# Two moves in a two-block transformer kernel: one projection issued a stage earlier, and the order of the first loads

## The reference

```python
h = _rms(x, attn_norm_g[l])
...
fq = _rms(_heads(proj("fox_q"), FOX_HEADS), fox_q_norm_g[l])    # 16 heads of 64
fk = _rms(_heads(proj("fox_k"), FOX_HEADS), fox_k_norm_g[l])
fv = _heads(proj("fox_v"), FOX_HEADS)
y_fox = _merge_heads(_fox_attention(fq, fk, fv, log_f))         # softmax attention with decay

def _rg_lru_branch(x, gate, conv_w, conv_b, w_a, b_a, w_x, b_x, lam):
    xc = _causal_dwconv(x, conv_w, conv_b)                      # x = proj("lru_x"), 4 taps
    r = sigmoid(einsum('bsnd,nde->bsne', xg, w_a) + b_a)        # xg: xc in 16 blocks of 64
    i = sigmoid(einsum('bsnd,nde->bsne', xg, w_x) + b_x)
    log_a = -LRU_C * r * softplus(-lam)
    ...
    return hs * gelu(gate)                                      # gate = proj("lru_g")

mem_n = _rms(mem, mem_norm_g[l])                                # read by the memory branch
```

## Time and profile before

| | before |
|---|---|
| runs (us) | 3090.07, 3090.10, 3087.36; median 3090.07 |
| the profiled execution: its own time | 3087.68 |
| its span | 3085.9 |
| PE busy | 3031.9 us, 98% of the span |
| DVE busy | 1628.8 us, 53% |
| ACT busy | 671.7 us, 22% |
| granted TensorE clock, mean | 0.999 |

### The profile page before, as it was taken

The page is one execution under the profiler, slowest core; times in us unless marked ns, Lnnn a source line. Parts: engine busy times, 40 slices in busy tenths (PEclk is TensorE's granted clock), DMA queues, the critical chain, the costliest instruction groups (busy, mean ns, idle before and its releaser), DMA issues.

```text
span 3085.9 us, 41509 instructions
## 1 busy us (share of the span) xinstructions
PE 3031.9 (98%) x13922; PEld 2419.9 (78%) x13922; DVE 1628.8 (53%) x3317; ACT 671.7 (22%) x1609; POOL 66.7 (2%) x109
## 2 busy tenths in 40 slices
PE   9999999999999999999999999999999999999998
PEld 8888888888885566767775588888866778887887
DVE  4456236666763466768886264444343666653111
ACT  3334210010003333311113041110053431022001
POOL 0000001100110000000000000000000000000000
PEclk9999999999999999999999999999999999999999
DMA  5243457756761111112221212222211223433443
GB/s 190 97 149 109 144 203 266 265 195 225 259 232 55 43 43 55 53 66 82 82 82 61 95 36 94 88 82 89 88 55 43 79 70 124 155 116 120 152 159 107
DMA packets 105001, 363.26 MB, mean 118 GB/s; under 512 B 11488, under 2 KB 17632, under 8 KB 104800
## 3 DMA queue, kind: packets, MB, share of 16 engines
q1 hardware_dynamic: 90832, 310.92, 29.5%
q0 software_dynamic: 14096, 51.39, 4.7%
HBM read 361.21 MB, written 1.05 MB: 117 GB/s over the span
## 4 chain that ended last, share of the span: by engine, by line
PE 95%; DVE 2%; issue 1%; ACT 1%; DMA 0%; DVEq 0%; ACTq 0%; SPq 0%
PE bank L569 42%; PE bank L942 6%; PE bank L1350 5%; PE bank L1010 4%; PE bank L1234 4%; PE bank L1125 3%; PE bank L580 3%; PE bank L842 2%; PE bank L1248 2%; PE bank L954 2%; PE bank L1098 2%; PE bank L1293 1%; PE bank L859 1%; PE bank L805 1%; PE bank L597 1%
## 5 line engine op out<-in xcount | busy, mean ns | idle before, releaser
L569 PE MATMUL bank<-H,W 128*128 128x256 f32 (+1 forms) x3488 | 816.3, 392 | 2.9 <-issue 2.8
L569 PEld LDWEIGHTS bank<-H,W 128*128 128x128 f32 x3488 | 661.4, 190 | 136.1 <-issue 52.0
L569 PE MATMUL bank<-YG,W 128*128 128x256 f32 (+1 forms) x1856 | 481.4, 416 | 1.8 <-issue 1.5
L569 PEld LDWEIGHTS bank<-YG,W 128*128 128x128 f32 x1856 | 352.8, 190 | 112.2 <-issue 72.5
L1125 PE MATMUL bank<-H,W 128*128 128x512 f32 (+1 forms) x320 | 119.7, 510 | 2.5 <-ACT H L1746 2.5
L1234 PE MATMUL bank<-W,H 128*128 128x256 f32 x512 | 117.1, 379 | 0.0
L1234 PEld LDWEIGHTS bank<-W,H 128*128 128x128 f32 x512 | 95.0, 191 | 13.1 <-issue 1.9
L942 PE MATMUL bank<-MX,SQ 128*128 128x256 f32 x480 | 105.2, 379 | 0.0
L1453 ACT ACT_TABLE_LOAD x21 | 26.9, 1283 | 346.4 <-DVEq L305 338.4
L942 PEld LDWEIGHTS bank<-MX,SQ 128*128 128x128 f32 x480 | 91.4, 190 | 12.2
L1125 PEld LDWEIGHTS bank<-H,W 128*128 128x128 f32 x320 | 58.7, 190 | 45.5 <-issue 37.0
(11 more groups left out here) (453 smaller groups left out, 4431.1 us busy)
## 6 DMA issues: line engine op xcount, KB each, us to landing
W<-stream SPq DMA_DIRECT2D x556, 512.0 KB, 3.3
WORK<-ada POOLq DMA_DIRECT2D x59, 512.0 KB, 4.0
SQ<-ada POOLq DMA_DIRECT2D x28, 512.0 KB, 5.5
W<-stream SPq DMA_DIRECT2D x24, 384.0 KB, 3.5
YG<-ada POOLq DMA_DIRECT2D x9, 512.0 KB, 4.6
W<-stream SPq DMA_DIRECT2D x16, 128.0 KB, 2.5
CN<-consts SPq DMA_DIRECT2D x1, 1984.0 KB, 15.4
X<-x_in SPq DMA_DIRECT2D x2, 512.0 KB, 5.1
```

What stands on the lines that cost most here:

```text
L569: m = pe.matmul(out_ap, W[u][:, c, :], src[:, c, cols], start=first and c == 0, stop=last and c == k - 1)
```

## The change

Three things. On SP, the small load of lambda is issued after the two halves of `x` instead of before them. On PE, projection 0 of the first `lru_in` turn is issued in `fox_last`, behind the transposes and ahead of the value products. And the body of `lru_in` on PE is cut anew: a turn has projection 1 and the block matmuls, and at its end projection 0 of the turn that follows; the last turn stands behind the loop. Two waits are added (`q_taken`, `k_taken` of the phases before), which guard banks 0 and 1 across the phases. ACT's and DVE's programs are not touched.

```diff
@@ block.sync
             lam = slice(PCOL["lru_lam"], PCOL["lru_lam"] + KC)
-            sp.dma_start(PR[:, lam], params[:, lam]).then_inc(tally.sem("lam_loaded"), 16)
             for h in range(2):
                 sp.dma_start(X[:, 4 * h:4 * h + 4, XS], x_in[:, 4 * h:4 * h + 4, :]).then_inc(tally.sem(f"x_loaded{h}"), 16)
+            sp.dma_start(PR[:, lam], params[:, lam]).then_inc(tally.sem("lam_loaded"), 16)
             sp.dma_start(CN[:, 0:EARLY_CONSTS], consts[:, 0:EARLY_CONSTS]).then_inc(tally.sem("consts_loaded"), 16)
@@ fox(s), on PE
                 if s.attends:
                     soft_transpose(pe, s, 0, bank[6], FOX_MOVES, 0)
                     soft_transpose(pe, s, 1, bank[5], FOX_MOVES, 0)
+                if not s.projects:
+                    lru_first(Step(tally, plan, s.number + 1, 0, counting=False))
                 if s.projects:
                     pe.wait_ge(*s.before("rstd"))
...
-            def lru_in(s):
+            def lru_first(s):
+                pe.wait_ge(*s.earlier("q_taken", 0))
                 pe.wait_ge(*s.before("conv_done"))
                 project(s, 0, bank[0][:, 0:S], XS)
+
+            def lru_begin(s):
+                pass
+
+            def lru_middle(s, following):
+                lru_rest(s)
+                lru_first(following)
+
+            def lru_rest(s):
+                pe.wait_ge(*s.earlier("k_taken", 0))
                 pe.wait_ge(*s.before("gate_taken"))
                 project(s, 1, bank[1][:, 0:S], XS)
                 pe.wait_ge(*s.done("loaded2"))
...
-            run(pe, {"prepare": prepare, "fox": fox, "lru_in": lru_in,
+            run(pe, {"prepare": prepare, "fox": fox, "lru_in": (lru_begin, lru_middle, lru_rest),
```

## The result

The changed kernel takes 3093.99 us (median of 16 runs, 3092.17 to 3096.62); the kernel before, with more runs than were shown ahead, 3088.65 us (16 runs, 3087.18 to 3090.10). The ratio is 1.0018, 95% interval [1.0011, 1.0025]: 5.3 us between the medians, slower, and on the edge of the 0.2% that I took as the bound of what can be told. The profiled execution took 3093.96 us.

The account below looks back on a forecast made before the run. The prediction took PE as the bound, busy for 3031.9 of 3085.9 us. Its terms 1.7 + 2.4 + 0 made +4.1 us on a median of 3090.07, so 3094.1 us, with a range from 3088.8 to 3097.0.

Parts of the forecast that it names:

- Part 1: First loads: lambda lands behind x, holding up ACT's squares and DVE's casts, so the normalisation starts late; +1.7 us.
- DVE's chain: At the start: DVE's work from lambda's landing to the last cast, 5.84 us, now ending at 12.64, later than ACT's root.
- Rival A: First loads: lambda lands by itself within 1.8 us of issue, start wins 0.45, seam loses 2.4; +1.9 us, chance 0.10.
- Part 2: Seam of fox_last and lru_in: early projection 0 overfills the 1.07 us hole, delaying value products and block matmuls; +2.4 us.
- DVE's series: At the seam: DVE's output copies, memory normalisation, clearing and convolution, behind the value products, hold the block matmuls; moves by 2.38.
- Part 3: lru_in loop cut anew: same PE order, turns stay 7.77 us and the loop's edge costs nothing; 0 us.
- rival C: lru_in loop: seven edges and one exit each show a PE issue gap, 3.5 us; +7.6 us in all, chance 0.12.
- Rival B: Start and seam: x comes 0.45 us earlier, the moved projection holds nothing up, seam wins nothing; -0.45 us, chance 0.05.

Follow-up runs that it names:

- e7: Kernel before plus the change's PE part, loads as before, with DVE's memory normalisation ahead of the output copies of fox_last; 3086.96 us, ratio 0.9993.
- e4: Kernel before plus the change's PE part, loads as before, with 7 unused matmuls ahead of projection 1; 3090.45 us, ratio 1.0004.
- e12: As e4, with 3 unused matmuls instead of 7 ahead of projection 1; one run, 3092.65 us.
- e3: Kernel before with only the lru_in loop cut anew, projection 0 of turn 0 kept behind the value products; 3087.38 us, ratio 0.9996.
- e8: Kernel before with only DVE's memory normalisation moved ahead of its output copies in fox_last; 3088.11 us, ratio 0.9997.
- e6: Kernel before with lambda's load issued on ACT's own queue and x first on SP; 3088.68 us, ratio 0.9999.
- e1: Kernel before with only lambda's load moved behind both halves of x on SP; 3090.31 us, ratio 1.0004.
- e10: Changed kernel with DVE's memory normalisation moved ahead of its output copies in fox_last; 3088.86 us, ratio 1.0001.
- e11: Kernel before with lambda's load between the halves of x, second trial of that kernel; one run, 3090.26 us.
- e2: Kernel before plus the change's PE part (early projection 0 and loop cut anew), loads as before; 3092.52 us, ratio 1.0011.

## Why the prediction came out

**The time.** 3094.1 forecast, 3093.99 measured, within the range, and the class (within 0.2%) as forecast, if narrowly. But the agreement to 0.1 us is luck: the median of before that I started from lay 1.4 us above that of 16 runs, and the loss was 5.3 and not 4.1. The two differences cancel almost exactly.

**Part 1 was right in its mechanism.** Lambda landed at 1.81 + 4.83 = 6.64, forecast 6.8. DVE's chain needed its 5.84 us from there and set the normalisation, not the root. The term was forecast at +1.7 and measured at +1.38: 0.16 from the landing, and the rest from the gap that I left between the casts and the normalisation, where the trace has them overlap (12.40, ahead of the last cast's end at 12.48). Half 0 of `x` landed at 0.75 + 4.1 = 4.85 and not at 5.35; nothing hung on that, since ACT waited for lambda anyway. The Trainium skill ("DMA: Bandwidth & Descriptors", section "Queues, rings and completion order") states that each DMA engine takes the descriptors of a ring in order. The traces agree: on SP's queue lambda landed at 5.1 and 5.3 behind half a megabyte and at 6.6 to 6.7 behind a whole one, and at 3.3 and 4.1 on a queue of its own. The fixed cost of some 2.0 us, which the prediction takes from the same page of the Trainium skill and which gave 3.8 us for lambda, does not hold behind `x`: lambda took 4.8 us there. In front, by itself, it had taken 1.8. Rival A, 1.8 us from the issue, is out; even on ACT's queue lambda took 2.5 and 3.3 us.

**Part 2 was right, down to the size, and incomplete.** The value products moved by 2.32 (forecast 2.38), the block matmuls by 2.34 (2.4), PE's stand was 3.46 (3.6). e7 shows that DVE's series was the reason. The step that failed is the end of that part of the prediction: I let PE stand for 3.6 us and gave the stand no price of its own beyond its length. The clock fell behind it and took another 1.69 us. It is missing in the sum and in the bounds, +2.6 to +5.0, and the 5.3 us lie outside these, if inside the wider range for the time. e4 (stand cut to 0.91 us, no fall) and e12 (2.63 us, fall) show that it is the stand. The first paragraph has the same error: with the matmuls unchanged, it says, a change can win or lose only within the 54 us that PE doesn't work. But PE's busy time itself grew by 3.1 us. A price stood in the trace of the kernel before, where PE stands for 2.88 us ahead of 2102.34 and then runs at half the clock for 3.4 us. PE in the timeline of the kernel before, and a stretch:

```profile
2102.34 9.94 PE L1010 MATMUL bank<-YG,W 128*128 128x256 f32 x37 [2.88 <-DVEq L305]
```

```profile
2104.00:2107.00 3.00, 3.00 (x9) 2.37 (x8) 2.96 (x2) 0.00 (x0) 0.00 (x0) 0.50 0.00 0
```

I had asked what the late work makes wait, and not what the waiting engine is like when it starts again.

**Part 3 was right.** e3 shows turns of 7.77 us; rival C is out.

**Rival B** named the bound that the repair runs into: with the value products on time nothing was to be won, for DVE's series and PE's work ended together. e7 and e8 bear that out from both sides: with DVE's job moved, the early projection is worth some 0.9 of the 1.2 us, and moving the job alone 0.3.

## What to carry to other kernels

A gap on the bounding engine is an offer only for work that fits into it: 3.45 us in a gap of 1.07 pushes whatever stands behind the gap, and if that feeds a long series on another engine, the bounding engine gets the time back as a stand. Shorten that series first. And look in the trace that you have for what the engine does behind a stand of that length: a stand can cost more than it lasts. And a load that looks unimportant because nobody waits long for it may be the first item in two engines' programs: before moving it back, ask how many bytes it will queue behind, and what each engine does in order after it.

## What the hardware showed that I had not expected

The granted clock of TensorE fell to half behind stands of 3.46, 3.50 and 2.63 us at the seam, for some 3.4 us each time, and stayed at full behind 0.91 us. By the clock records of these three traces it fell 0.3 to 1.4 us after PE had started again. But the length of the stand alone does not decide. The stand of 2.9 us near 2100 us is in all fourteen traces; in thirteen the clock falls there (3.4 us at half, 6.8 in e4 and e12), in e6 it stays at 1.00. And both kernels have a stand of 2.30 us near 2400 us, in the same work. PE in the timeline of the changed kernel there, and two stretches:

```profile
2407.03 0.68 PE L1306 MATMUL bank<-WORK 128*128 128x128 f32 x4 [2.30 <-DVE WORK L2615]
```

```profile
2407.00:2409.00 2.00, 1.97 (x9) 1.77 (x10) 2.00 (x5) 1.12 (x5) 0.00 (x0) 0.76 0.03 8
2409.00:2412.00 3.00, 3.00 (x11) 2.59 (x11) 1.85 (x7) 2.56 (x9) 0.00 (x0) 0.59 0.00 0
```

In the trace of the kernel before, the same stand ends at 2401.48 and the clock stays at 1.00; of the other twelve traces e1, e3, e10 and e11 have the fall there (a granted clock of 0.93 over the stretch from 2390 to 2415), the other eight have 1.00. By the chains of waits the changed kernel is 5.55 us behind at 2398 and 6.91 us at 2434. Nor does the place in time sort them: in e3 the same stand ends 0.13 us later than in the kernel before and has the fall, in e6 0.76 us later and has none. So a fall worth 1.4 us can be there in one trace and absent in another, far from the edit, and that is of the size of the effects studied here; with one trace of each kernel, such a piece can't be put down to the edit. At the seam three kernels agree, and so do the medians of e2 and e4, 2.1 us apart. What decides whether the clock falls behind stands of 2.3 to 2.9 us was not tried.

And a 4 KB transfer between two of 512 KB delayed the second, twice: half 1 of `x`, issued at 1.8, landed at 8.1 and 8.4 us. Issued at 1.7 in the order of before, it landed at 7.1 to 7.3 in seven traces. Issued at 1.26, right behind half 0 and with lambda after it, it landed at 6.4 in the changed kernel.
